# Retention with a decay split per key and per query, one root for three norms, and the fourth retrieval in one piece

## The chip, the cores and the metric

The kernel runs on one core of a Trainium2 chip. The metric is the device time of one execution in microseconds (us). TensorE (PE) does matmuls, VectorE (DVE) and ScalarE (ACT) elementwise work and reductions, GpSimd (POOL) issues the indirect DMAs that gather expert rows, and SyncE (SP) issues the plain ones. The engines run side by side and wait for each other through semaphores.

## What is computed

A decoder layer over 512 tokens of width 1024: a mixer of four retention heads and four differential attention heads, a layer norm, then PEER, a retrieval of 128 of 16384 experts per token (8 heads, 16 each), and a second layer norm. Cut to what matters:

```python
# retention, per head, chunks of 128 tokens, g the head's decay
s = (q_i k_j^T) * decay_in          # g^(i-j), 0 for i < j
out = s v_j + (q_i state) * decay_q # state: all earlier chunks, decayed
r = silu(gate) * GroupNorm(out)     # eps 1e-5, over the 128 values of a head
# attention
a = softmax(q1 k1^T) - lam * softmax(q2 k2^T)
d = 0.8 * RMSNorm(a v)
x = LayerNorm(alpha * x + concat(r, d) @ W_out)
# PEER, per token
top = top16 of the sums of two top16 lists of 128 key scores
h = gelu(x . U[expert]);  y = sum(softmax(score) * h * V[expert])
x = LayerNorm(alpha * x + y)
```

## The kernel before

The 512 tokens are four blocks of 128, one token per partition. Block 0 goes ahead alone: projections, retention, attention, layer norm and its retrieval. From then on GpSimd gathers the experts of block 0, while TensorE does projections, retention and attention of blocks 1 to 3. At last come the queries and retrieval of these blocks, and the gather of their 384 experts per partition.

**The gather of block 0.** An expert's row is 4 KB of U and 4 KB of V; one indirect DMA brings one row for each of the 128 tokens (512 KB). `U k` is a group of four such transfers, rows 4k to 4k+3 (here "rows"), and `V j` likewise. They land in a ring of 16 slots, four quads A to D, and a slot is filled anew only when its row has been used (`slot_used`). GpSimd issues in the fixed order of `ROWS`: U0 to U19 in quads A and B by turns; then, once the last retention product is done (`ret_mixed` 4, since quads C and D lie in buffers of the retention), V0 U20 V1 U21 V2 U22 V3 U23 V4 U24 U25 V5 U26 U27 V6 U28 U29 U30 V7 U31 V8 V12 V9 V13 and so on. From there V0 to V11 use C and A by turns, even U use D, odd U use B, V12 uses D, V13 B. VectorE takes each U row with a dot product with x (`dot`, L1120, 128x1024), in order, wherever its program says `rows(n)`. V0 to V11 are summed by TensorE (`add_rows`, L529) with a diagonal matrix of weights that ScalarE makes (L964); V12 and later by VectorE (`weighed_sum`, L1134).

**Projections of blocks 1 to 3.** The order is rotated queries and keys (RQ, RK), RV, the gate RG, then DQ, DKK, DV for attention, the last three as 4 + 4 + 3 fills. A fill waits until its bank, used three fills before, has been read: the second and third DQ fill wait for VectorE's gate (`swish_gate`, L1264) of blocks 2 and 3. Beside the rotations and gates VectorE takes rows and the retrievals 2 and 3 of block 0: the loop counter `i` runs over nine fills, retrieval 2 stands at i = 5, and `best_keys(0, 3)` alone at i = 6, behind the first gate. Between the DQ, DKK and DV fills TensorE does retention: scores of query block b against key block jb into ACC (L710), and the product with v into W[:, 3] (L720), in the steps of the list `RETENTION`.

**Retention on VectorE.** `decay_scores` scales each tile of scores with a table that holds the whole decay g^(i-j); tiles two or three blocks off the diagonal take four instructions, one for each head. `retention_norm` of a block has statistics, a root by three Newton steps, the norm of four heads out of PSUM, gain, bias and the gate. It stands behind each block's product, and the product of the next block waits for it (`ret_normed`), since all use one bank. Then `weights(0)` makes the first V weights from the gelu that ScalarE has computed ahead of its last projection copy.

**Attention.** For each block b and head h VectorE masks the scores and takes their maximum (`softmax_max`), takes `BESIDE_HEAD[b]` rows, and joins the two softmaxes (`softmax_join`). In block 1, heads 1 and 2 have one row each, beside `best_pairs` and `best_experts` of the fourth retrieval. For blocks 2 and 3, head 2 has two rows and the layer norm `ln1` of the block before. After the heads come four rows, `diff_norm(b)` and `AFTER_NORM[b]` rows. TensorE has for each head the scores of the next head, one V group (block 1: V0 to V3, and V4 behind the heads), the transposes of this head's probabilities, and the product; the last row of the V group stands between transposes and product. A block ends with the turning of the normed mix (L783) and the scores of the next block.

## Time and profile before

| | us |
|---|---|
| median of 3 runs | 1594.28 (1594.04 to 1595.39) |
| profiled execution | 1593.78 |
| its span | 1592.0 |
| busy PE / DVE / ACT / POOL | 1288.4 / 1123.6 / 271.6 / 737.2 |
| DMA | 603.45 MB, mean 379 GB/s |

The profiled execution is 0.5 us under the median, and 1.8 us of it lie outside the span from the first to the last instruction. Busy shares are means over the whole span. An engine that is idle for half of it can still be the one that all wait for in a stage, so the table is read together with windows of time and the idle time in front of an instruction.

### The profile page before, as it was taken

The numbers are of one execution on the slowest core, as the hardware profiler recorded it, in microseconds if no ns is written. First come the engines' busy times: TensorE is split into PE (matmuls) and PEld (weight loads), VectorE is DVE, ScalarE is ACT, GpSimd is POOL, SyncE is SP. The second block draws the span as 40 slices with busy tenths as digits, with TensorE's granted clock in tenths as the row PEclk, the third lists the DMA queues.
The fourth block names the chain that finished last, engine by engine and source line by source line (L and its number), as shares of the span: only waits on it lengthen the run. The fifth ranks groups of instructions, "written<-read, shape, count | busy, mean of one in ns | idle before, by whom it ended". The sixth has DMA issues, their size and how long they took to land.

```text
span 1592.0 us, 11574 instructions
## 1 busy us (share of the span) xinstructions
PE 1288.4 (81%) x3512; PEld 619.0 (39%) x3512; DVE 1123.6 (71%) x2626; ACT 271.6 (17%) x771; POOL 737.2 (46%) x645
## 2 busy tenths in 40 slices
PE   8999989977678995788787777778787868778787
PEld 5466446433334563333233333333333323333232
DVE  1459999777787967987676768676767686755555
ACT  0200100212122110121212121212121212121111
POOL 0006475767656456454444443535353444344430
PEclk9999989998889998899989898979998899899988
DMA  9859898989889989999999999999999999999994
GB/s 349 352 216 390 296 364 298 412 289 341 286 295 348 351 329 416 381 421 422 421 422 422 421 421 421 422 422 421 421 422 421 421 422 421 422 421 422 421 422 177
DMA packets 100254, 603.45 MB, mean 379 GB/s; under 512 B 11616, under 2 KB 11872, under 8 KB 47584
## 3 DMA queue, kind: packets, MB, share of 16 engines
q0 software_dynamic: 92160, 536.91, 83.7%
q1 hardware_dynamic: 8032, 65.80, 10.3%
q8 instruction: 28, 0.46, 0.1%
q14 instruction: 34, 0.28, 0.0%
HBM read 600.57 MB, written 2.10 MB: 379 GB/s over the span
## 4 chain that ended last, share of the span: by engine, by line
DMA 43%; PE 22%; DVE 21%; POOL 7%; issue 4%; ACT 1%; SPq 1%; DVEq 0%; POOLq 0%
DMA arena<-uv,idx 41%; PE W L542 7%; POOL arena L505 5%; DVE arena L1142 4%; PE ACC L542 4%; PE W L580 3%; PE W L586 3%; PE W L828 2%; DVE arena L1120 2%; DVE xs L1134 2%; DMA arena<-w_in 1%; PE ACC L529 1%; PE X L664 1%; PE X L795 1%; DVE cand L1405 1%
## 5 line engine op out<-in xcount | busy, mean ns | idle before, releaser
L1142 DVE SCALAR_TENSOR_TENSOR arena<-arena,xs 128x1024 f32<-128x1024 f32 x384 | 466.9, 1226 | 293.2 <-DMA arena<-uv,idx 291.4
L489 POOL DMA_INDIRECT arena<-uv,idx x384 | 426.8, 1112 | 530.2 <-PE W L542 310.8
L542 PE MATMUL W<-arena,fdiag 128*128 128x512 f32 x1024 | 494.2, 642 | 144.0 <-ACT fdiag L1072 143.9
L505 POOL DMA_INDIRECT arena<-uv,idx x232 | 282.0, 1216 | 265.3 <-DVE idx L1412 116.9
L542 PEld LDWEIGHTS W<-arena,fdiag 128*128 128x128 f32 x1024 | 206.9, 206 | 430.7 <-issue 249.7
L542 PE MATMUL ACC<-arena,fdiag 128*128 128x512 f32 x512 | 252.8, 655 | 70.4 <-ACT fdiag L1072 70.3
L542 PEld LDWEIGHTS ACC<-arena,fdiag 128*128 128x128 f32 x512 | 105.6, 210 | 217.5 <-issue 131.5
L1072 ACT ACTIVATE fdiag<-ident,gate 128x128 f32<-128x128 f32 x384 | 123.6, 390 | 340.1 <-DVE gate L1150 329.8
L1120 DVE SCALAR_TENSOR_TENSOR arena<-arena,xs 128x1024 f32<-128x1024 f32 x128 | 150.4, 1223 | 22.2 <-DMA arena<-uv,idx 20.8
L580 PE MATMUL W<-arena 128*128 128x512 f32 x272 | 122.7, 605 | 8.7 <-DMA arena<-w_in 8.1
L1134 DVE SCALAR_TENSOR_TENSOR xs<-arena,gate,xs 128x1024 f32<-128x1024 f32 x80 | 102.7, 1284 | 33.4 <-DMA arena<-uv,idx 26.5
L828 PE MATMUL W<-arena 128*128 128x128 f32 (+1 forms) x512 | 112.7, 381 | 1.5 <-ACT arena L1014 1.5
L1064 ACT ACTIVATE hid<-hid 128x4 f32<-128x4 f32 (+2 forms) x101 | 20.7, 205 | 427.5 <-DVE arena L1142 427.5
L828 PEld LDWEIGHTS W<-arena 128*128 128x128 f32 x512 | 77.4, 191 | 35.8 <-ACT arena L1014 2.0
L580 PEld LDWEIGHTS W<-arena 128*128 128x128 f32 x272 | 51.5, 194 | 69.1 <-issue 65.6
L586 PE MATMUL W<-arena 128*128 128x128 f32 (+1 forms) x256 | 61.5, 399 | 7.8 <-issue 4.3
L529 PE MATMUL ACC<-arena,fdiag 128*128 128x512 f32 x96 | 47.5, 645 | 9.1 <-DMA arena<-uv,idx 6.3
L586 PEld LDWEIGHTS W<-arena 128*128 128x128 f32 x256 | 40.3, 199 | 26.5 <-issue 13.3
L795 PE MATMUL X<-arena 128*128 128x512 f32 x96 | 47.1, 641 | 1.6 <-issue 1.6
L1142 DVE DVE_READ_ACCUMULATOR arena<-arena,xs 128x1 f32 x384 | 31.6, 82 | 0.0
L529 PEld LDWEIGHTS ACC<-arena,fdiag 128*128 128x128 f32 x96 | 18.9, 206 | 31.3 <-issue 24.1
L1031 ACT ACTIVATE arena<-W 128x384 f32<-128x384 f32 (+1 forms) x20 | 10.2, 512 | 116.1 <-PE W L828 109.6
(198 smaller groups left out, 896.6 us busy)
## 6 DMA issues: line engine op xcount, KB each, us to landing
arena<-w_in SPq DMA_DIRECT2D x13, 2048.0 KB, 18.6
arena<-peer_w_query SPq DMA_DIRECT2D x8, 2048.0 KB, 19.8
arena<-uv,idx POOLq DMA_INDIRECT x616, 29.1
arena<-w_out SPq DMA_DIRECT2D x4, 2048.0 KB
arena<-w_in SPq DMA_DIRECT2D x4, 512.0 KB, 6.7
arena<-xT SPq DMA_DIRECT2D x1, 1536.0 KB, 11.8
xs<-x SPq DMA_DIRECT2D x1, 1536.0 KB, 14.6
out<-xs SPq DMA_DIRECT2D x3, 512.0 KB
```

The costliest lines, as they stand in the source:

```text
L489: pool.indirect_dma_start(out=fused[slot], out_offset=None, in_=uv, in_offset=bass.IndirectOffsetOnAxis(ap=idx[:, E + n:E + n + 1], axis=0 ...
L505: pool.indirect_dma_start(out=ring[r], out_offset=None, in_=rows, in_offset=bass.IndirectOffsetOnAxis(ap=idx[:, e:e + 1], axis=0), element ...
L529: last = nc.tensor.matmul(ACC[:, half * HW:(half + 1) * HW], fdiag[:, i % ND, :], ring[r][:, half * HW:(half + 1) * HW], start=i == 0, sto ...
L542: last = nc.tensor.matmul(sum_of(b)[:, half * HW:(half + 1) * HW], fdiag[:, n % ND, :], fused[n % NS][:, D + half * HW:D + (half + 1) * HW ...
L580: last = nc.tensor.matmul(bank, act_T(k, part * P, (part + 1) * P), wts[slot][:, k, :], start=(k == 0), stop=(k == KD - 1))
L586: last = nc.tensor.matmul(bank[:, at:at + n_tok], wts[slot][:, k, h * P:(h + 1) * P], act_T(k, toks.start, toks.stop), start=(k == 0), sto ...
L795: last = nc.tensor.matmul(X_BANKS[half], mixT[:, k, :], wts[slot_of_out(half)][:, k, :], start=(k == 0), stop=(k == KD - 1))
L828: last = nc.tensor.matmul(dst, wts[slot][:, k, i * P:(i + 1) * P], act_T(k, toks.start, toks.stop), start=(k == 0), stop=(k == KD - 1))
L1072: nc.scalar.activation(fdiag[:, n % ND, :], ident[:], ACT.Copy, scale=gate[:, E + n:E + n + 1]).then_inc(pair_diag_ready, 1)
L1120: STT(out=ring[r], in0=ring[r], scalar=1.0, in1=xs[:, 0, :], op0=ALU.mult, op1=ALU.mult, accum_out=hid[:, e:e + 1]).then_inc(slot_used[r], 1)
L1134: STT(out=xs[:, 0, :], in0=ring[r], scalar=gate[:, e:e + 1], in1=xs[:, 0, :], op0=ALU.mult, op1=ALU.add).then_inc(slot_used[r], 1)
L1142: STT(out=fused[slot][:, 0:D], in0=fused[slot][:, 0:D], scalar=1.0, in1=xs[:, b, :], op0=ALU.mult, op1=ALU.mult, accum_out=hid[:, E + n:E ...
```

## The change

Four things are changed.

- The decay g^(i-j) is split. The factor of the query is left out, since a norm follows that divides each row by its own size, and the norm's epsilon is multiplied by the square of what was left out (`row_eps`). What remains depends on the key alone: on the diagonal a table with the mask (`near`, still VectorE's), off it one number per key and head (`across`), which ScalarE applies as the scale of a copy (`scale_scores`, 24 pieces of 128x128 behind copies of projections).
- The products of blocks 1, 2 and 3 go to three banks (`RET_BANKS`), so none waits for a norm. VectorE takes only statistics for each, then one root for all three. ScalarE applies scale and bias in 12 pieces of 128x128, behind its last projection copy, and VectorE multiplies by gain, adds the bias and gates in three instructions over 1536 elements (`retention_gate`). The first maximum of attention stands behind these.
- The fourth retrieval of block 0 stands whole at i = 6, between the first two gates.
- The rows are dealt out anew: 28 in place of 24 beside retention, 5 beside each head of blocks 1 and 2 (2 at head 2 of block 2), none after the norm of block 1.

```diff
-BESIDE_HEAD = {1: 5, 2: 6, 3: 4}
-AFTER_NORM = {1: 8, 2: 3, 3: 11}
+BESIDE_HEAD = {1: 5, 2: 5, 3: 4}
+AFTER_NORM = {1: 0, 2: 3, 3: 11}
...
+        near = part(5 * K, HW)
+        across = part(5 * K + HW, 3 * H, "p (o h) -> p o h", o=3)
+        eps_in = part(5 * K + HW + 3 * H, H)
...
+        row_eps = sb("row_eps", [P, H])
+        ret_mv = work[:, 0:6 * H].rearrange("p (q h c) -> p q h c", q=3, h=H)
+        ret_scale = work[:, 6 * H:9 * H]
+        ret_bias = work[:, 9 * H:12 * H]
+        ret_root = work[:, 12 * H:18 * H].rearrange("p (i n) -> p i n", i=2)
+        ret_out = attn[:, :].rearrange("p (q n) -> p q n", q=3)
...
+        RET_BANKS = [W[:, 3, :], X_BANKS[0], X_BANKS[1], W[:, 3, :]]
...
-                        pe.wait_ge(ret_decayed, tiles_before(NB))
+                        pe.wait_ge(ret_decayed, NB)
+                        pe.wait_ge(ret_scaled, tiles_before(NB - 1))
                     pe.wait_ge(row_landed[r], landed(p))
...
             def retention_mix(b):
-                pe.wait_ge(ret_decayed, tiles_before(b + 1))
-                if b > 1:
-                    pe.wait_ge(ret_normed, b)
+                pe.wait_ge(ret_decayed, b + 1)
+                if b:
+                    pe.wait_ge(ret_scaled, tiles_before(b))
                 for h in range(H):
                     for jb in range(b + 1):
-                        last = nc.tensor.matmul(W[:, 3, h * P:(h + 1) * P], sT[:, jb, h * P:(h + 1) * P],
+                        last = nc.tensor.matmul(RET_BANKS[b][:, h * P:(h + 1) * P], sT[:, jb, h * P:(h + 1) * P],
                                                 rv[:, jb, h * P:(h + 1) * P], start=(jb == 0), stop=(jb == b))
                 last.then_inc(ret_mixed, 1)
...
                     pe.wait_ge(a_ready, n + 1)
                     if b == 1 and h == 0:
-                        pe.wait_ge(ret_normed, NB)
+                        pe.wait_ge(ret_applied, 1)
                     else:
...
+                    for b, jb in OFF_TILES.get(fill[0] - 1 - fill_of(1, RG) - 1, ()):
+                        scale_scores(b, jb)
+                act.wait_ge(ret_scales_ready, 1)
+                for q in range(3):
+                    for h in range(H):
+                        n = q * H + h
+                        last = nc.scalar.activation(ret_out[:, q, h * P:(h + 1) * P], RET_BANKS[q + 1][:, h * P:(h + 1) * P],
+                                                    ACT.Identity, bias=ret_bias[:, n:n + 1], scale=ret_scale[:, n:n + 1])
+                last.then_inc(ret_applied, 1)
+            OFF_TILES = {1: [(1, 0)], 3: [(2, 0), (2, 1)], 6: [(3, 0), (3, 1)], 7: [(3, 2)]}
+            def scale_scores(b, jb):
+                act.wait_ge(ret_scored, tiles_before(b) + jb + 1)
+                act.wait_ge(ret_mixed, b)
+                if b == 1:
+                    act.wait_ge(proj_taken_dve, takes(len(FILLS), "dve"))
+                src = ACC[:, jb % 2 * HW:(jb % 2 + 1) * HW]
+                for h in range(H):
+                    last = nc.scalar.activation(sT[:, jb, h * P:(h + 1) * P], src[:, h * P:(h + 1) * P], ACT.Copy,
+                                                scale=across[:, b - jb - 1, h:h + 1])
+                last.then_inc(ret_scaled, 1)
...
-            def decay_scores(b, jb):
-                off = b - jb
-                dve.wait_ge(ret_scored, tiles_before(b) + jb + 1)
-                src = ACC[:, jb % 2 * HW:(jb % 2 + 1) * HW]
-                if off < 2:
-                    TT(out=sT[:, jb, :], in0=src, in1=dec[:, off, :], op=ALU.mult).then_inc(ret_decayed, 1)
-                else:
-                    for h in range(H):
-                        ins = STT(out=sT[:, jb, h * P:(h + 1) * P], in0=src[:, h * P:(h + 1) * P],
-                                  scalar=decay_far[h] ** (off - 1), in1=dec[:, 1, h * P:(h + 1) * P],
-                                  op0=ALU.mult, op1=ALU.mult)
-                    ins.then_inc(ret_decayed, 1)
...
-            def retention_norm(b):
-                R = W[:, 3, :]
-                q = b - (b > 0)
-                dve.wait_ge(ret_mixed, b + 1)
+            def decay_scores(b):
+                dve.wait_ge(ret_scored, tiles_before(b) + b + 1)
+                src = ACC[:, b % 2 * HW:(b % 2 + 1) * HW]
+                TT(out=sT[:, b, :], in0=src, in1=near, op=ALU.mult).then_inc(ret_decayed, 1)
+            def retention_norm_0():
+                R = RET_BANKS[0]
+                dve.wait_ge(ret_mixed, 1)
                 links([nc.vector.bn_stats(st[:, h, :], R[:, h * P:(h + 1) * P]) for h in range(H)])
                 links([nc.vector.bn_aggr(mv[:, h, :], st[:, h, :]) for h in range(H)])
-                link(TS(rstd[:], mv[:, :, 1], EPS, None, ALU.add))
-                inverse_root(rstd[:], H)
+                link(TT(out=rstd[:], in0=mv[:, :, 1], in1=row_eps[:], op=ALU.add))
+                inverse_root(rstd[:], H, root)
                 for h in range(H):
                     ins = TS(work[:, h * P:(h + 1) * P], R[:, h * P:(h + 1) * P], mv[:, h, 0:1], rstd[:, h:h + 1],
                              ALU.subtract, ALU.mult)
-                    if h == H - 1:
-                        ins.then_inc(ret_normed, 1)
-                dve.wait_ge(ret_normed, b + 1)
+                ins.then_inc(ret_normed, 1)
+                dve.wait_ge(ret_normed, 1)
                 link(TT(out=work[:, 0:HW], in0=work[:, 0:HW], in1=gn[:, 0, :], op=ALU.mult))
                 link(TT(out=work[:, 0:HW], in0=work[:, 0:HW], in1=gn[:, 1, :], op=ALU.add))
-                if b:
-                    link(TT(out=swish[:, q, :], in0=work[:, 0:HW], in1=swish[:, q, :], op=ALU.mult))
+            def retention_statistics(b):
+                R = RET_BANKS[b]
+                dve.wait_ge(ret_mixed, b + 1)
+                links([nc.vector.bn_stats(st[:, h, :], R[:, h * P:(h + 1) * P]) for h in range(H)])
+                links([nc.vector.bn_aggr(ret_mv[:, b - 1, h, :], st[:, h, :]) for h in range(H)])
+            def retention_scales():
+                by_block = ret_scale.rearrange("p (q h) -> p q h", q=3)
+                link(TT(out=by_block, in0=ret_mv[:, :, :, 1], in1=row_eps[:].unsqueeze(1).to_broadcast([P, 3, H]), op=ALU.add))
+                inverse_root(ret_scale, 3 * H, ret_root)
+                STT(out=ret_bias.rearrange("p (q h) -> p q h", q=3), in0=ret_mv[:, :, :, 0], scalar=-1.0, in1=by_block,
+                    op0=ALU.mult, op1=ALU.mult).then_inc(ret_scales_ready, 1)
+            def retention_gate():
+                dve.wait_ge(ret_applied, 1)
+                for i, op in ((0, ALU.mult), (1, ALU.add)):
+                    link(TT(out=ret_out, in0=ret_out, in1=gn[:, i, :].unsqueeze(1).to_broadcast([P, 3, HW]), op=op))
+                link(TT(out=swish[:], in0=ret_out, in1=swish[:], op=ALU.mult))
...
-                if i == 5:
-                    retrieve(0, 2)
-                elif i == 6:
-                    best_keys(0, 3)
+                if i in (5, 6):
+                    retrieve(0, i - 3)
             dve.wait_ge(rot_turned, rots(len(FILLS)))
             rows(HALF)
-            for b in range(1, NB):
-                for jb in range(b + 1):
-                    decay_scores(b, jb)
-                    if jb % 2:
-                        rows(HALF)
-                if b > 1:
-                    rows(HALF)
-                retention_norm(b)
+            decay_scores(1)
+            rows(HALF)
+            retention_statistics(1)
+            rows(HALF)
+            decay_scores(2)
+            rows(HALF)
+            retention_statistics(2)
+            rows(HALF)
+            decay_scores(3)
+            rows(2 * HALF)
+            retention_statistics(3)
+            retention_scales()
             weights(0)
+            rows(HALF)
+            retention_gate()
             for b in range(1, NB):
                 for h in range(H):
                     softmax_max(b, h)
                     if b > 1 and h == 2:
                         rows(2)
                         ln1(b - 1)
-                    elif (b, h) == (1, 1):
-                        best_pairs()
-                        rows(1)
-                    elif (b, h) == (1, 2):
-                        best_experts(0, 3)
-                        rows(1)
                     else:
...
-    decay = (np.stack([near, far], axis=1) * P ** -0.5).reshape(P, 2, HW)
+    left = np.exp((P - 1 - i)[:, None] * log_g[None, :]) * P ** -0.5
+    near = (i[None, None, :] >= i[:, None, None]) * left[:, :, None]
+    across = left[:, None, :] * np.exp(P * np.arange(1, NB)[None, :, None] * log_g[None, None, :])
+    row_eps = EPS * np.exp(2.0 * (P - 1 - i)[:, None] * log_g[None, :])
+    decay = np.concatenate([near.reshape(P, -1), across.reshape(P, -1), row_eps], axis=1)
     ang = np.arange(S)[:, None] * (10000.0 ** (-np.arange(64) / 64.0))[None, :]
     rope = np.stack([np.cos(ang), np.sin(ang)]).reshape(2, NB, P, 64).transpose(2, 0, 1, 3).reshape(P, -1)
```

On VectorE between the gates of blocks 1 and 2, before (L1264 is the gate, L1375 to L1379 `best_keys`, L1120 the dots):

```order
L1264 SCALAR_TENSOR_TENSOR arena<-arena,W 128x512
L1375 MAX best_v<-arena 128x8 x4
L1376 MATCH_REPLACE cand<-best_v,arena 128x128 x4
L1377 MAX_INDEX best_i<-best_v,arena 128x8 x4
L1378 MAX best_v<-cand 128x8 x4
L1379 MAX_INDEX best_i<-best_v,cand 128x8 x4
L1120 SCALAR_TENSOR_TENSOR arena,hid<-arena,xs 128x1024 x8
```

And the same place after the change, from the last step of `best_keys` to the second gate (L1433 to L1442 `best_pairs`, L1449 to L1461 `best_experts`):

```order
L1428 MAX_INDEX best_i<-best_v,cand 128x8 x4
L1433 TENSOR_TENSOR cand<-best_v 128x512
L1438 MAX top_v<-cand 128x8 x2
...
L1452 TENSOR_TENSOR cand<-pos_u,iota_f 128x1024
L1454 TENSOR_TENSOR cand<-cand,best_i 128x1024
L1455 TENSOR_REDUCE sel<-cand 128x64
...
L1461 SCALAR_TENSOR_TENSOR idx<-sel 128x32
L1160 SCALAR_TENSOR_TENSOR arena,hid<-arena,xs 128x1024 x8
L1304 SCALAR_TENSOR_TENSOR arena<-arena,W 128x512
```

The eight dots and the second and third gate now stand behind thirteen more kinds of instruction.

On VectorE at the end of retention, before (L1296 to L1304 end the norm of block 3, L1168 to L1172 are `weights(0)`, L1310 begins attention):

```order
L1296 TENSOR_SCALAR arena<-W,mv,rstd 128x128 x4
L1301 TENSOR_TENSOR arena<-arena 128x512
L1302 TENSOR_TENSOR arena<-arena 128x512
L1304 TENSOR_TENSOR arena<-arena 128x512
L1168 TENSOR_REDUCE gsum<-gate 128x4
L1169 RECIPROCAL gsum<-gsum 128x4
L1170 TENSOR_TENSOR gate<-gate,gsum 128x64
L1172 TENSOR_TENSOR gate<-gate,hid 128x64
L1310 TENSOR_TENSOR W<-W,mask 128x2x128
```

And after the change (L1345 makes the biases of the norms, L1352 and L1353 are `retention_gate`):

```order
L1345 SCALAR_TENSOR_TENSOR arena<-arena 128x12
L1208 TENSOR_REDUCE gsum<-gate 128x4
L1209 RECIPROCAL gsum<-gsum 128x4
L1210 TENSOR_TENSOR gate<-gate,gsum 128x64
L1212 TENSOR_TENSOR gate<-gate,hid 128x64
L1160 SCALAR_TENSOR_TENSOR arena,hid<-arena,xs 128x1024 x4
L1352 TENSOR_TENSOR arena<-arena 128x1536 x2
L1353 TENSOR_TENSOR arena<-arena 128x1536
L1359 TENSOR_TENSOR W<-W,mask 128x2x128
```

Four dots and the gate of all three blocks now stand between the weights and the first maximum.

On ScalarE after the change, at the end of the projections (L931 a projection copy, L1088 and L1091 the exponential and gelu for `weights(0)`, L977 the norm's pieces, L1014 the first exponentials of attention):

```order
L931 ACTIVATE arena<-W 128x512 x2
L1088 ACTIVATE gate<-gate 128x64
L1091 ACT_TABLE_LOAD
L1091 ACTIVATE hid<-hid 128x64
L931 ACTIVATE arena<-W 128x512
L977 ACTIVATE arena<-X,arena 128x128 x8
L977 ACTIVATE arena<-W,arena 128x128 x4
L1014 ACT_TABLE_LOAD
L1014 ACTIVATE arena,zsum<-W,nmax 128x256 x2
```

The twelve pieces are new. They stand behind the copy of the last projection and ahead of the table load of attention.

## Rows read from the trace of the kernel before

**Rows 1.** The page: chain of waits that ended last, by engine.

```profile
DMA 43%; PE 22%; DVE 21%; POOL 7%; issue 4%; ACT 1%; SPq 1%; DVEq 0%; POOLq 0%
```

**Rows 2.** Windows: stretch, length; PE, PEld, DVE, ACT, POOL busy; clock, DMA share, GB/s.

```profile
229.00:297.70 68.70, 68.57 (x272) 42.81 (x272) 59.51 (x159) 5.82 (x11) 45.76 (x37) 0.96 0.90 340
...
300.60:361.60 61.00, 46.08 (x128) 21.51 (x128) 49.90 (x118) 13.41 (x50) 39.73 (x34) 0.91 0.87 326
361.60:432.90 71.30, 50.24 (x136) 24.08 (x136) 54.57 (x119) 15.51 (x46) 51.62 (x43) 0.86 0.86 310
...
570.00:1580.00 1010.00, 794.46 (x1726) 343.43 (x1725) 684.63 (x1593) 183.26 (x535) 445.99 (x403) 0.90 1.00 414
```

**Rows 3.** Timeline of TensorE: start, length, line, operation, idle before and releaser.

```profile
215.95 7.09 PE L586 MATMUL W<-arena 128*128 128x384 f32 x16 [3.45 <-DVE arena L1264]
...
229.13 7.89 PE L586 MATMUL W<-arena 128*128 128x384 f32 x16 [4.31 <-issue]
...
302.32 5.40 PE L529 MATMUL ACC<-kT,fdiag 128*128 128x512 f32 x8
...
309.49 1.88 PE L529 MATMUL ACC<-rv,fdiag 128*128 128x512 f32 x4
...
355.55 1.04 PE L783 MATMUL W<-ident,arena 128*128 128x128 f32 x8
```

**Rows 4.** Timeline of VectorE: the fourth retrieval and what follows its parts.

```profile
308.72 0.75 DVE L1384 TENSOR_TENSOR cand<-best_v 128x512 f32<-128x512 f32 x1
...
313.84 1.22 DVE L1120 SCALAR_TENSOR_TENSOR arena<-arena,xs 128x1024 f32<-128x1024 f32 x1
...
317.49 0.26 DVE L1400 TENSOR_SCALAR pos_u<-top_p 128x32 uint32<-128x32 uint32 x2
317.79 1.23 DVE L1403 TENSOR_TENSOR cand<-pos_u,iota_f 128x1024 f32<-128x1024 uint32 x1
...
322.11 1.22 DVE L1120 SCALAR_TENSOR_TENSOR arena<-arena,xs 128x1024 f32<-128x1024 f32 x1
```

**Rows 5.** Timeline of VectorE: a norm of retention, then tiles of the next block.

```profile
239.27 0.89 DVE L1291 BATCH_NORM_STATS2 st<-W 128x6 f32<-128x128 f32 x4
...
240.60 0.17 DVE L1293 TENSOR_SCALAR rstd<-mv 128x4 f32<-128x4 f32 x1
...
243.00 1.37 DVE L1296 TENSOR_SCALAR arena<-W,mv,rstd 128x128 f32<-128x128 f32 x4
...
246.58 0.88 DVE L1281 SCALAR_TENSOR_TENSOR arena<-ACC,arena 128x128 f32<-128x128 f32 x4
247.38 0.68 DVE L1277 TENSOR_TENSOR arena<-ACC,arena 128x512 f32<-128x512 f32 x1
```

**Rows 6.** Timeline of ScalarE: four diagonals of V0.

```profile
301.53 1.27 ACT L964 ACTIVATE fdiag<-ident,gate 128x128 f32<-128x128 f32 x4
```

**Rows 7.** Timeline of GpSimd: transfers, with idle time before and releaser.

```profile
284.87 0.98 POOL L505 DMA_INDIRECT kT<-uv,idx  x1 [0.30 <-issue]
...
323.61 0.93 POOL L505 DMA_INDIRECT arena<-uv,idx  x1 [7.33 <-DVE arena L1120]
327.25 1.68 POOL L505 DMA_INDIRECT arena<-uv,idx  x1 [2.71 <-DVE arena L1120]
...
385.07 0.94 POOL L505 DMA_INDIRECT arena<-uv,idx  x1 [0.30 <-issue]
...
405.43 1.68 POOL L505 DMA_INDIRECT arena<-uv,idx  x1 [7.17 <-DVE arena L1120]
...
561.53 1.73 POOL L489 DMA_INDIRECT arena<-uv,idx  x1 [16.01 <-DVE idx L1412]
```

**Rows 8.** Timeline of VectorE: three waits in attention.

```profile
346.40 0.17 DVE L1347 TENSOR_SCALAR rstd<-ssq 128x4 f32<-128x4 f32 x1 [9.02 <-ACT arena L998]
...
390.65 1.22 DVE L1120 SCALAR_TENSOR_TENSOR arena<-arena,xs 128x1024 f32<-128x1024 f32 x1 [1.66 <-DMA arena<-uv,idx]
...
445.77 4.06 DVE L1134 SCALAR_TENSOR_TENSOR xs<-arena,gate,xs 128x1024 f32<-128x1024 f32 x3 [4.34 <-DMA arena<-uv,idx]
```

35 lines of the change are left out of this document (19 added, 16 removed).

## The prediction

> **What bounds the kernel now.** I read four views. The chain of waits says where time can be given back: transfers of expert rows hold 43% of it, TensorE 22%, VectorE 21% [rows 1]. The table of windows then gives the stages. From 570 us on the DMA engines are full to the end (share 1.00 over 1010 us, 414 GB/s [rows 2]), and the bytes are fixed. So the end moves with one instant: the issue of the first row of block 1, at 561.53 us, for which GpSimd had waited 16.01 us [rows 7]. What the change can do is move that instant. It is reached through attention of blocks 1, 2 and 3, then layer norm and queries, a chain that the change doesn't touch behind 433 us.
>
> Ahead of it the timelines of each engine matter, because no engine is full everywhere. From 229 to 297.7 TensorE has 68.57 us of work in 68.70 us [rows 2], and its start there, at 229.13 us, follows an idle 4.31 us for which the row names no engine; the fill reuses the bank of the last gate, as the one at 215.95 us, behind 3.45 us of waiting for VectorE, reuses that of the gate before [rows 3]. In attention of block 1, GpSimd stops for 7.33 and 2.71 us at 323.61 and 327.25 us, since VectorE does retrieval instead of using rows; TensorE then lacks V rows and VectorE waits 9.02 us at 346.40 us [rows 7, 8]. There is another stop of 7.17 us at 405.43 us [rows 7].
>
> **The change on VectorE.** Removed: three norms of 7.3 us (239.27 to 246.58 [rows 5]), 21.9 us; the scaling of the six off-diagonal tiles, three in four instructions (0.88 us in all) and three in one (0.68 us [rows 5]), less overlap about 4.2 us. Added: three times statistics (239.27 to 240.60, 1.3 us), 3.9 us; one root over 12 columns, as long as the one over 4, with bias, 2.6 us (240.6 to 243.0 plus one step [rows 5]); three operations over 1536 elements. The trace has 1.23 us for 1024 elements [rows 4], so about 1.8 us each, 5.4 us. The saving is 26.1 - 11.9 = 14.2 us. Row dots are only moved: both kernels have done 128 of them by the norm of block 2.
>
> **The fourth retrieval.** Its pairs (308.72 to 313.84, 5.1 us) and experts (317.49 to 322.11, 4.6 us) [rows 4] leave attention of block 1, and stand between the first and second gates of block 1 to 3. That is 9.7 us ahead of the last gate, on which TensorE waits. Ends: +9.7 us if the loop "row used, next transfer issued, landed" moves as a whole; +6.3 us if all landings are then hidden, because eight dots of 1.15 us are 9.2 us, where the stretch from gate to gate took 13.2 us (215.95 to 229.13 [rows 3]), 0.7 us of it a gate. A transfer needs 5.6 us from issue to landing (385.07 to 390.65 [rows 7, 8]), and since the first of the eight is issued only when the first of the eight before it is used, the 3.4 us of landing waits mostly stay; I take +9.0 us. TensorE has no gap behind it to absorb this. It ends the projections at 297.7 + 9.0 = 306.7 us, and the last retention product, which frees the buffers of the V rows, moves from 284.87 [rows 7] to 293.9 us. VectorE's 14.2 us are not lost to work but to waiting: its diagonal tiles of blocks 2 and 3 must wait for TensorE's scores, which now come 9 us later, while VectorE comes earlier. ScalarE's six scaled tiles are 24 pieces, 7.6 us by [rows 6], where it has 5.82 us of work in 68.7 us [rows 2]; each is behind the copy of a projection and done within 2.6 us, while TensorE is in the next projection of over 5 us. I cost them at nothing; without that cover it would be up to 2.6 us for each of three blocks.
>
> **The new wait.** ScalarE applies the three norms behind its last projection copy, so not before TensorE's 306.7 us, although the scales are ready at about 297 us (third product 293 us, statistics 1.3, root 2.6). Copy 0.6 us, then 12 pieces. Nearest row: four scaled copies of the same size in 1.27 us [rows 6], so 3.8 us; bounds 2.4 us (0.2 each, under the rate of that row) and 6 us (0.5 each). ScalarE is done at 311.1 us. VectorE is held at retention_gate, has 5.4 us there, and behind it is queued the first maximum of attention, for which TensorE, ScalarE and the V rows wait. It ends at 316.5 + 1.4 = 318 us against 300.6 us: 17.4 us late.
>
> A rule of the Trainium skill bears on this price: "ScalarE: Activation LUTs", section "What ACT_TABLE_LOAD costs", has 186 ns and 0.833 ns per column for an activation, 93 ns more for each per-partition operand, and an overlap of 93 ns. For one such operand that makes 1.27 us for four, as the row; the new pieces have two, a scale and a bias, and would need 4.7 us, which would put all that follows 0.9 us later.
>
> **Attention of block 1.** GpSimd's order of transfers is unchanged: V0 U20 V1 U21 V2 U22 V3 U23 V4 U24 U25. V0 starts at 293.9, U21 is out at about 315 us. V2 takes the slots of V0, and TensorE takes V0 only behind the first maximum: 1.7 us behind it, 5.40 us for two rows and 1.88 us for each further one [rows 3]. So V2 goes out from 324 to 330 us: a stop of some 8 us, in the place of the 7.33 and 2.71 us that go. From then on the heads run in lockstep with the stream. Each head now wants five new U rows, up to a group that is issued behind V(h+2), whose last slot is freed behind the join of head h: 2.3 us (transposes and one V row of 1.88 us), one issue and one to three more of 1.25 us, landing 5.6 us, a dot and a join of 2.4 us: 12.9, 14.2 and 15.4 us, against the 8.8 us of a head before (308.72 and 317.49, behind the second and third maximum [rows 4]). Joins end at 325, 338, 352 and 367 us. U25, four rows on, lands by 373 us; norm 3.6 us. V4 on TensorE (four rows, 7.2 us) ends at 382.5 us, and from the turning at 355.55 us [rows 3] to the maximum at 361.6 us it was 6.0 us: block 2 starts at 388.5 us, 26.9 us late, with four dots more behind it.
>
> **Attention of block 2.** Before: 71.3 us, of which VectorE was busy 54.57 us [rows 2]. Four dots fewer are 50.0 us, and rows now lie ready because the stream has gone on: 388.5 + 50.0 = 438.5 us, 5.6 us late where it was 26.9. The stop of 7.17 us at the layer norm gets shorter too, since all of U28 is used ahead of it (BESIDE_HEAD 5 and four rows in hand).
>
> **Attention of block 3.** Before, VectorE waits there 4.34 us for V rows at 445.77 us [rows 8]. The stream at that place (V8, V9, V12, V13) is late by 0 to 2 us only, so the wait takes up 4.3 of the 5.6 us; TensorE, late by some us more, gives back a part. I take +2 us, which goes through 561.53 us to the end. The profiled execution took 1593.78 us; with +2 us it is 1595.8. The median of the runs shown, 1594.28, is 0.5 us above it: 1596.3 us.
>
> Bounds of this case: with +6.3 us in place of +9.0 the delay at 433 us is 2.9 us and is wholly taken up, about -0.5 us in all. If TensorE is still at the V row before when a head's join comes, its last one is freed 1.9 us later [rows 3], and the three heads cost 5 us more: +6 us. So 1593.8 to 1600.5 us.
>
> **Rivals.**
> Stream first, faster. If GpSimd doesn't stop for V2 and the heads don't hold it, the stream starts 9 us late (V0), but drops the stops of 7.33, 2.71 and most of 7.17 us: 9 - 17 = -8 us, 1586 us. For it: the DMA share in 300.6 to 432.9 us is only 0.87 and 0.86 [rows 2], so up to 18 us are there to be had, and the freed VectorE time is 14.2 us. Against it: V2 can't be issued until V0 is used, and that is behind the wait for ScalarE.
>
> Start of attention not given back, slower. The wait of 4.34 us in block 3 takes up the delay only if V12 and V13 aren't late. They reuse slots of the last U rows, dotted in block 2. If the lockstep lasts into block 2 (V5 and V6 wait for heads of it, and V7 is summed ahead of the turning), these slots are freed 6 to 8 us late, and nothing is taken up: 1601.5 us. It decides once block 2 ends over 6 us late.
>
> The saving counts in full: VectorE's 14.2 us go straight into the chain, 1580 us. Only 21% of the chain is VectorE's, and TensorE's full stretch speaks against it.
>
> **How the numbers follow.** Forecast 0.50 (of it 0.39 same, 0.09 slower, 0.02 faster); stream first 0.24; not given back 0.23; in full 0.03. What this measurement can tell from no change is 0.2%, 3.2 us. Of each of the first two rivals 0.03 is same. Faster: 0.21 + 0.03 + 0.02 = 0.26. Same: 0.39 + 0.06 = 0.45. Slower: 0.20 + 0.09 = 0.29. The range goes from 1586.5 to 1602 us.
>
> **What would show it.** TensorE's last projection at 304 to 307 us instead of 297.7; ScalarE's 12 pieces behind it, 3 to 5 us; VectorE idle at retention_gate for some 4 us and the first maximum at 315 to 318 us; GpSimd stopped for TensorE near 320 us and not for VectorE; heads of 12 to 15 us; block 2 from 380 or later; a shorter wait than 4.34 us in block 3; the first row of block 1 at 562 to 566 us. It is wrong if block 2 starts before 372 us, if the last gate is late by less than 5 us, or if the time from 570 us on changes.

## The result, and the profile after

The changed kernel takes 1610.27 us (median of 4 runs, 1607.85 to 1610.74) against 1594.49 us of the kernel before beside it: ratio 1.0099, 95% interval 1.0087 to 1.0112. It is 15.8 us slower where I had forecast +2, and lies above my range. The profiled execution took 1607.85 us, its span is 1605.9, so the traces have 13.9 us of the loss. All ratios of this document leave out one execution of 1620.94 us, of the kernel before with the retrieval moved, which was in a slower state of the chip; the median of 1600.18 us given for that kernel counts it (1599.63 without).

The windows of the changed kernel, cut at the last projection, the gate, the first maximum of block 2, the norm of block 2 and the first row of block 1 (columns as in [rows 2]):

```profile
229.00:303.70 74.70, 71.72 (x296) 45.32 (x294) 52.64 (x118) 12.93 (x36) 48.63 (x44) 0.98 0.96 353
303.70:314.00 10.30, 0.70 (x4) 0.30 (x4) 5.93 (x6) 6.06 (x14) 7.66 (x6) 0.68 1.01 418
314.00:391.00 77.00, 51.67 (x128) 23.86 (x128) 41.40 (x93) 13.53 (x50) 42.55 (x42) 0.80 0.81 292
391.00:444.00 53.00, 45.44 (x136) 21.86 (x136) 50.41 (x113) 15.40 (x46) 35.85 (x29) 0.94 0.84 292
444.00:575.00 131.00, 113.09 (x356) 58.87 (x355) 109.06 (x185) 25.93 (x65) 74.31 (x66) 0.95 0.86 321
575.00:1605.00 1030.00, 806.03 (x1759) 350.23 (x1757) 699.52 (x1619) 184.24 (x537) 456.39 (x408) 0.90 0.99 409
```

Attention of block 1 lasts 77 us where it had 61 [rows 2], and VectorE works 41.40 us of it instead of 49.90. The retrieval's 9.7 us have left this stage, so VectorE has less to do here and is idle for 35.6 us where it was for 11.1. From 575 us on the DMA engines are full, as in [rows 2].

GpSimd in the changed kernel, start, length and idle before each transfer (the stops, the rows issued behind them, and the first row of block 1):

```profile
290.21 0.94 POOL L517 DMA_INDIRECT kT<-uv,idx  x1 [2.15 <-PE W L737]
...
321.53 0.97 POOL L517 DMA_INDIRECT kT<-uv,idx  x1 [8.64 <-PE ACC L542]
...
342.27 0.93 POOL L517 DMA_INDIRECT arena<-uv,idx  x1 [4.77 <-PE ACC L542]
343.51 0.94 POOL L517 DMA_INDIRECT arena<-uv,idx  x1 [0.30 <-issue]
...
345.99 0.94 POOL L517 DMA_INDIRECT arena<-uv,idx  x1 [0.30 <-issue]
...
359.24 0.94 POOL L517 DMA_INDIRECT rv<-uv,idx  x1 [6.99 <-PE ACC L542]
...
425.37 0.94 POOL L517 DMA_INDIRECT arena<-uv,idx  x1 [2.71 <-PE ACC L542]
...
452.18 0.94 POOL L517 DMA_INDIRECT arena<-uv,idx  x1 [0.30 <-issue]
...
575.52 1.74 POOL L501 DMA_INDIRECT arena<-uv,idx  x1 [15.66 <-DVE idx L1461]
```

The two stops for VectorE in block 1 (7.33 and 2.71 us in [rows 7]) are gone, and the one of 7.17 us in block 2 has shrunk to 0.89 and 1.97 us (402.57 and 412.21). In their place GpSimd waits for TensorE: for the first slot of V2 (321.53), then for the last slot of V3, of V4 and of V5 (2.48 us at 377.48), and in block 2 for the last slot of V7 (425.37), behind which it issues without a stop up to the first row of V13 (452.18). The first row of block 1 comes at 575.52 us, 13.99 late: the instant that the prediction had named carries the loss.

VectorE in the changed kernel, the gate and the waits:

```profile
308.52 3.55 DVE L1352 TENSOR_TENSOR arena<-arena 128x1536 f32<-128x1536 f32 x2 [4.26 <-ACT arena L977]
312.11 1.76 DVE L1353 TENSOR_TENSOR arena<-arena 128x1536 f32<-128x1536 f32 x1
313.90 0.43 DVE L1359 TENSOR_TENSOR W<-W,mask 128x256 f32<-128x256 f32 x1
...
333.77 1.22 DVE L1160 SCALAR_TENSOR_TENSOR arena<-arena,xs 128x1024 f32<-128x1024 f32 x1 [6.86 <-DMA arena<-uv,idx]
...
348.82 1.23 DVE L1160 SCALAR_TENSOR_TENSOR arena<-arena,xs 128x1024 f32<-128x1024 f32 x1 [7.13 <-DMA arena<-uv,idx]
...
352.53 1.22 DVE L1160 SCALAR_TENSOR_TENSOR arena<-arena,xs 128x1024 f32<-128x1024 f32 x1 [1.09 <-DMA arena<-uv,idx]
353.69 0.16 DVE L1368 RECIPROCAL rz<-zsum 128x2 f32<-128x2 f32 x1
...
365.70 1.23 DVE L1160 SCALAR_TENSOR_TENSOR arena<-arena,xs 128x1024 f32<-128x1024 f32 x1 [8.29 <-DMA arena<-uv,idx]
...
390.77 0.43 DVE L1359 TENSOR_TENSOR W<-W,mask 128x256 f32<-128x256 f32 x1 [7.75 <-PE W L753]
...
442.86 1.13 DVE L1399 SCALAR_TENSOR_TENSOR arena<-W,rstd,arena 128x128 f32<-128x128 f32 x4
446.87 2.67 DVE L1174 SCALAR_TENSOR_TENSOR xs<-arena,gate,xs 128x1024 f32<-128x1024 f32 x2 [2.88 <-DMA arena<-uv,idx]
...
458.12 1.29 DVE L1174 SCALAR_TENSOR_TENSOR xs<-arena,gate,xs 128x1024 f32<-128x1024 f32 x1 [4.06 <-DMA arena<-uv,idx]
```

The wait for ScalarE (4.26 us) and the gate stand ahead of the first maximum. Then each of three heads has one long wait for a U row. Block 3's wait for V rows, 4.34 us in [rows 8], is still 4.06 us although VectorE comes 12 us later.

### The profile page after: what moved, and what is told of

The parts are those of the page before. It is cut to its first block, busy times and chain, and to the rows that moved or that the text cites. A ratio compares the mean times of both kernels' runs of the same rounds, so it can differ in the third digit from the quotient of the medians.

```text
span 1605.9 us, 11561 instructions
## 1 busy us (share of the span) xinstructions
PE 1291.9 (80%) x3512; PEld 620.7 (39%) x3512; DVE 1110.9 (69%) x2571; ACT 282.2 (18%) x807; POOL 732.0 (46%) x645
## 3 DMA queue, kind: packets, MB, share of 16 engines
q1 hardware_dynamic: 8032, 65.55, 10.2%
## 4 chain that ended last, share of the span: by engine, by line
DMA 43%; PE 26%; DVE 20%; POOL 4%; issue 3%; ACT 2%; SPq 1%; DVEq 0%; POOLq 0%
DMA arena<-uv,idx 42%; PE W L555 8%; DVE arena L1182 4%; POOL arena L517 3%; PE ACC L555 3%; PE ACC L542 3%; PE W L593 3%; PE W L845 2%; PE W L599 2%; PE X L812 2%; DVE arena L1160 2%; DVE xs L1174 2%; DMA arena<-w_in 1%; PE X L677 1%; DVE top_p L1439 1%
## 5 line engine op out<-in xcount | busy, mean ns | idle before, releaser
L555 PEld LDWEIGHTS ACC<-arena,fdiag 128*128 128x128 f32 x512 | 106.8, 213 | 217.4 <-issue 133.3
L599 PE MATMUL W<-arena 128*128 128x128 f32 (+1 forms) x256 | 62.0, 401 | 15.4 <-DVE arena L1304 15.4
L753 PE MATMUL W<-dkT,arena 64*128 64x256 f32 (+2 forms) x48 | 13.2, 632 | 25.4 <-ACT arena L1014 23.2
L1071 ACT ACTIVATE arena<-W 128x384 f32<-128x384 f32 (+1 forms) x20 | 10.2, 512 | 116.1 <-PE W L845 116.1
## 6 DMA issues: line engine op xcount, KB each, us to landing
xs<-x SPq DMA_DIRECT2D x1, 1536.0 KB, 14.2
```

Source lines behind the costliest of these rows:

```text
L555: last = nc.tensor.matmul(sum_of(b)[:, half * HW:(half + 1) * HW], fdiag[:, n % ND, :], fused[n % NS][:, D + half * HW:D + (half + 1) * HW ...
L599: last = nc.tensor.matmul(bank[:, at:at + n_tok], wts[slot][:, k, h * P:(h + 1) * P], act_T(k, toks.start, toks.stop), start=(k == 0), sto ...
```

## The experiments

Theory GROUP, formed from these rows: U groups of four rows are issued in the order U20 V1 U21 V2 U22 V3 U23 V4 U24. A head's dots need the rows up to some group. With 80 rows used ahead of attention and 5 beside each head, head h (0 to 3) reads into U(21+h). For heads 1 to 3 that group is issued behind V(h+1), which takes the slots of V(h-1), and the last of these is freed behind the join of head h-1. So each head waits until the join before it has passed through TensorE, GpSimd and a landing. (The expectations count from the head whose join frees the slot, and so say V(h+2).) With 76 rows ahead a head reads into U(20+h), one group less. The rivals: START (the late first maximum passes whole to the end), ROWS or HEADS (five rows beside a head are too many anyway), DECAY (the decays and norms on ScalarE cost it).

Each ratio below is to the kernel before, run on the same chip. The chips differ between groups of experiments, and a ratio can be 0.1% off the quotient of the two medians (1606.88 by 1596.76 gives 1.0063 where the ratio is 1.0049), so differences of that size are not read. "Moved retrieval" means pairs and experts of the fourth quarter.

**Undoing one part, or doing it alone.** First, retrieval and rows of block 1 as before:

```diff
-                if i in (5, 6): retrieve(0, i - 3)
+                if i == 5: retrieve(0, 2)
+                elif i == 6: best_keys(0, 3)
+                    elif (b, h) == (1, 1): best_pairs(); rows(1)
+                    elif (b, h) == (1, 2): best_experts(0, 3); rows(1)
-AFTER_NORM = {1: 0, 2: 3, 3: 11}
+AFTER_NORM = {1: 8, 2: 3, 3: 11}
```

> The changed kernel (median 1610.27) with its fourth retrieval put back where it was: best keys between the first two gates, pairs and experts beside the second and third head of block 1; the rows beside those heads and behind the norm go back with it (5, 1, 1, 5, 8), everything else of the change stays. Theory START (the late start of attention, 14.7 us at the first maximum, goes through whole; about 6 of it come from the retrieval ahead of the last gate and 8.7 from the norms that wait for ScalarE): last projection at 297, first maximum at 307 to 309, and a time of 1602 to 1604. Theory HEADS (the five rows beside each head of block 1 wait for transfers; the start matters little): heads as before, 1593 to 1597. Theory DECAY (the scaled tiles and norms on ScalarE cost the time): no gain, 1608 or more.

Measured: 1592.92 us, ratio 0.9976 (0.9952 to 1.0000), against 1.0099. START can't be the whole: its first maximum comes 7.3 us late (306.51 against 299.22), and its time is no longer than that of the kernel before. (The profiled execution, 1596.71 us, is a long one of this kernel: its block 3 begins at 435.40 us, 2.95 early, and its first row comes at 564.55, 3.0 late; the last section has 2.6 us of what lies between.) DECAY fell: the new decays and norms are in it.

The other way round, the kernel before with the retrieval moved and the rows of block 1 dealt 5 and 0:

> The kernel before (median 1594.5) with only the fourth retrieval moved in one piece between the first two gates, and rows dealt as in the changed kernel in block 1 (5 beside each head, none behind the norm). Decays and norms are the old ones. START: the last projection ends 6 to 9 us late, so does the first maximum, and that goes through: 1600 to 1604. HEADS: lockstep heads on top of it, the whole loss of the change is here: 1607 to 1611. DECAY: 1593 to 1597.

Measured: 1600.18 us, ratio 1.0031 (0.9998 to 1.0065). That is at the low edge of START, since the kernel before had 1596.76 on this chip. But this move costs only some 5 us here by the ratio (3.4 by the medians, and the interval reaches 1), and undoing it in the changed kernel gained over 15. The effects don't add; something in the changed kernel makes it dear. The difference is that the changed kernel has used 80 rows ahead of attention, and this one 76. Adding them ahead, and taking them from block 2 as the change does:

```diff
             weights(0)
+            rows(HALF)
             for b in range(1, NB):
-BESIDE_HEAD = {1: 5, 2: 6, 3: 4}
+BESIDE_HEAD = {1: 5, 2: 5, 3: 4}
```

> The kernel before with the fourth retrieval in one piece and all of the changed kernel's dealing of rows (80 rows ahead of attention, 5 beside each head of blocks 1 and 2, none behind the norm of block 1); decays and norms are the old ones. It differs from the one-piece kernel measured at 1600.2 against 1596.8 by those four rows. GROUP: heads of block 1 go from 11 us to 14 to 17 and the time to 1606 to 1610 by the scale on which the kernel before has 1596.8. START: the first maximum moves by at most 2 us, so does the time: 1600 to 1603. A time like the changed kernel's (over 1609) would mean that the new decays and norms cost nothing and bring nothing.

Measured: 1606.84 us against 1593.61, ratio 1.0085 (1.0056 to 1.0113). Its first maximum (309.72) is only 2.7 us later than with 76 rows (307.06), its last join of block 1 begins 29 us later (374.88 against 345.94). With old decays and norms this is nearly all of the loss.

**The same four rows in the changed kernel.**

```diff
             weights(0)
-            rows(HALF)
             retention_gate()
-AFTER_NORM = {1: 0, 2: 3, 3: 11}
+AFTER_NORM = {1: 4, 2: 3, 3: 11}
```

> The changed kernel with four row dots taken from ahead of attention (behind the statistics of block 3) and put behind the norm of block 1: 76 rows are used before the first maximum, as in the kernel before, instead of 80. Retrieval, decays and norms stay as changed. Theory GROUP (80 rows ahead plus five beside each head make every head of block 1 need a group of U rows whose transfers are issued behind V(h+2), a V row whose slot comes free behind the join of the head itself; with 76 each head needs one group less): waits for DMA in the heads fall from about 7 to 2 to 4.5 us, the heads from 15 to 18 us to 11 to 12, the maximum of block 2 from 390.8 to 375 to 381, time 6 to 11 below the changed kernel, 1600 to 1605 by the clock of its first measurement (kernel before 1594.5). Theory START (only the late first maximum counts): time within 2 us of the changed kernel. Theory ROWS (five rows beside each head are too many, wherever one starts): heads stay at 15 us or more, within 2 us too.

Measured: 1601.55 us, ratio 1.0050 (1.0030 to 1.0070). Four dots, moved and not saved, give back a third to a half of the loss (0.0025 of the 0.0075 that the changed kernel has in its second measurement below, 0.0049 of the 0.0099 in its first). VectorE's waits in the heads of this kernel:

```profile
340.01 1.23 DVE L1160 SCALAR_TENSOR_TENSOR arena<-arena,xs 128x1024 f32<-128x1024 f32 x1 [3.40 <-DMA arena<-uv,idx]
350.70 1.23 DVE L1160 SCALAR_TENSOR_TENSOR arena<-arena,xs 128x1024 f32<-128x1024 f32 x1 [3.04 <-DMA arena<-uv,idx]
361.81 1.23 DVE L1160 SCALAR_TENSOR_TENSOR arena<-arena,xs 128x1024 f32<-128x1024 f32 x1 [4.45 <-DMA arena<-uv,idx]
```

They were 6.86, 7.13 and 8.29 us; the first maximum of block 2 comes at 375.69 us instead of 390.77. GROUP holds. ROWS, by which the five beside a head stay too many, falls.

GROUP says more: with 80 rows ahead and 4 beside each head the last groups read are the same as with 76 and 5. With the changed kernel again beside it:

> The changed kernel with 4 rows beside each head of block 1 in place of 5 and the 4 rows so taken behind its norm; the 80 rows ahead of attention stay. Theory GROUP: what counts is the last group of U rows that a head reads (head h then reads U(20+h), as with 76 rows ahead and 5 beside each, where the ratio was 1.005; the changed kernel's heads read U(21+h)): waits for DMA of 2 to 5 us in a head instead of 7, block 2's first maximum at 373 to 380, ratio 1.003 to 1.006. Rival AHEAD (80 rows used before attention drain the ring, and the rows beside a head don't matter): ratio 1.008 or more. Rival ROWS (only the number beside a head matters): 1.000 to 1.003, below the kernel with four rows later.

> The changed kernel itself again, on the chip of the three kernels that run beside it, so that they can be compared with it directly. A ratio to the kernel before of 1.009 to 1.011, as at first (1.0099).

Measured: 1595.42 us, ratio 1.0017 (1.0003 to 1.0032), and the changed kernel 1605.95 us, 1.0075 (1.0051 to 1.0098), below the 1.009 to 1.011 that I expected of it. AHEAD fell clearly, and the first maximum of block 2 (374.64 us) is where GROUP put it. The ratio is below what I expected of GROUP and within that of ROWS (1.000 to 1.003), so one row less beside a head is worth some more than its group. How much can't be said: the interval meets that of the kernel with four rows later, at 1.0030.

**Place of the retrieval, and of the norms.** Pairs and experts can stand where VectorE waits for TensorE in any case:

```diff
             rows(HALF)
+            best_pairs()
             decay_scores(2)
 ...
             rows(HALF)
+            best_experts(0, 3)
             decay_scores(3)
```

> The changed kernel with pairs and experts of the fourth retrieval taken from between the gates and put into two stretches in which VectorE waits for TensorE's retention scores (4.66 us at 257.80 and 7.88 us at 279.54); best keys stay ahead of the last gate, rows as in the changed kernel. START: last gate 7 us earlier, last projection at 297, first maximum at 307 to 309, time 1602 to 1604, as with the old place of the retrieval. HEADS: five rows beside each head stay, so the heads stay in lockstep with the transfers and little is gained: 1607 to 1610. The two kernels with the retrieval out of the gates differ under HEADS by 10 us and under START by less than 2.

Measured: 1601.43 us, ratio 1.0020 (1.0001 to 1.0040). Nearer to START than to HEADS, and by the ratio below both, though the heads stayed in lockstep: waits of 7.58, 7.05 and 8.39 us, block 2 at 387.15 us. So the retrieval ahead of the gate costs some us of its own: by the traces 4.8 at the first row (570.76 against 575.52), by the ratios more (0.0055 to 0.0079). What is left, 0.0044 against the old retrieval (0.9976), is the dealing of block 1 together with the place of pairs and experts; no run here parts the two.

ScalarE's twelve pieces ahead of its last projection copy:

```diff
                     if fill[0] == len(FILLS) - 1:
                         gelu_0(0)
+                        apply_norms()
                     take_fill(1, WAVES[1])
```

> The changed kernel with ScalarE's twelve norm pieces issued ahead of its last projection copy instead of behind it, so that they lie beside TensorE's last projection. START: pieces at about 299 to 304, three operations of VectorE behind them, first maximum at 309 to 310.5 instead of 313.9, time 3.5 to 4.5 lower, 1606 to 1607. HEADS: the heads wait for transfers all the same, under 1.5 us gained, 1609 or more. DECAY: like START, since the wait is ScalarE's.

Measured: 1606.88 us, ratio 1.0049 (1.0018 to 1.0079). From the last projection's end to the first maximum it was 10.2 us (303.67 to 313.90); here it is 5.8 (307.72 to 313.52), the 4.4 us foreseen. Against the changed kernel's two measurements, 1.0075 and 1.0099, the gain is 0.0026 and 0.0050, where START had 0.0022 to 0.0028. The interval overlaps that of the first of these and not that of the second, so the size stays open. In the profiled execution TensorE was 4 us later to begin with, and the first row comes 1.7 us earlier (573.81 against 575.52). The same edit where the heads are free:

> The changed kernel with the retrieval and the rows of block 1 put back as before, and ScalarE's twelve norm pieces ahead of its last projection copy. The first maximum comes 4.4 us earlier than without the latter (306.5), at 302. GROUP: no lockstep in these heads, so VectorE sets them and the 4.4 us count at least in part: 2 to 4.5 us below the kernel with only the old retrieval, which is 6 to 8 us below the kernel before (ratio 0.995 to 0.996). START: 4.4 us in full. The rival DECAY, by which the new norms bring nothing, has it within 2 us of the kernel before.

Measured: 1585.36 us, ratio 0.9949 (0.9934 to 0.9963): 4.3 us (0.0027) below the same without the edit, as expected, though the two intervals still meet, and clearly faster than the kernel before.

**Together.** The retrieval in the waits, the norms earlier, the four rows behind the norm:

> Three edits of the changed kernel at once: pairs and experts of the fourth retrieval in VectorE's waits of the retention stage, the norm pieces ahead of ScalarE's last copy, and the four row dots behind the norm of block 1. First maximum at 302. GROUP: heads of about 10 to 11 us, block 2 from 352 to 358, 5 to 9 us below the kernel before (ratio 0.9945 to 0.997). ROWS: five rows beside each head hold the heads at 15 us or more: at or above the kernel before. START: 1594 to 1597 by the scale on which the kernel before has 1594.5.

Measured: 1586.49 us, ratio 0.9952 (0.9936 to 0.9967). Then with fewer rows beside each head (`BESIDE_HEAD` 4 and 3 for block 1, `AFTER_NORM` 8 and 12):

> The kernel with the retrieval in the waits, the norms earlier and 76 rows ahead (ratio 0.9952), with 4 rows beside each head of block 1 and 8 behind its norm in place of 5 and 4. Head h then reads U(19+h). GROUP: the waits of 4.17, 2.52 and 3.71 us in its heads shrink to under 2 us each, but the rows come behind the norm instead, where TensorE's V4 lies beside them: 0 to 4 us lower, ratio 0.993 to 0.9955. Rival TAIL (what the heads gain is lost at the V rows that block 3 needs): same within 1 us.

> The same with 3 rows beside each head and 12 behind the norm. GROUP: no wait for DMA in the heads, which last as long as their V rows on TensorE, 8.3 us; behind the norm VectorE has 12 dots, 14 us, beside TensorE's V4 and block 2's first scores, and is now the later: block 2's first maximum at 352 to 358; ratio 0.991 to 0.996, no clear difference from 4 and 8.

Measured: with 4 rows 1581.20 us, ratio 0.9924 (0.9901 to 0.9947); with 3 rows 1584.88 us, 0.9947 (0.9931 to 0.9963). The version with 4 is 12.2 us faster than the kernel before and the lowest of the three; its interval meets those of the other two, so the order among them isn't settled. VectorE's waits of over 0.5 us for U rows in it, from the first maximum of block 1 to the end of block 2:

```profile
336.53 1.23 DVE L1164 SCALAR_TENSOR_TENSOR arena<-arena,xs 128x1024 f32<-128x1024 f32 x1 [4.10 <-DMA arena<-uv,idx]
339.85 1.22 DVE L1164 SCALAR_TENSOR_TENSOR arena<-arena,xs 128x1024 f32<-128x1024 f32 x1 [0.67 <-DMA arena<-uv,idx]
347.75 1.22 DVE L1164 SCALAR_TENSOR_TENSOR arena<-arena,xs 128x1024 f32<-128x1024 f32 x1 [1.95 <-DMA arena<-uv,idx]
364.87 1.22 DVE L1164 SCALAR_TENSOR_TENSOR arena<-arena,xs 128x1024 f32<-128x1024 f32 x1 [4.40 <-DMA arena<-uv,idx]
381.35 1.23 DVE L1164 SCALAR_TENSOR_TENSOR arena<-arena,xs 128x1024 f32<-128x1024 f32 x1 [3.52 <-DMA arena<-uv,idx]
```

All come behind the last join of block 1, whose joins begin 7.4 to 8.4 us apart (307.99 to 331.07). With 3 rows the heads have no wait for a transfer either, and block 2 starts at 360.15 us instead of 358.84, later than the 358 that I gave as a bound; which of its waits sets that I did not settle.

**Does block 3's wait take up a delay?** Eight operations without effect (128x512, `max(x, x)`) were put into the kernel before on VectorE, ahead of the first maximum of block 3, or of block 2; and seven of 1024 elements ahead of the very first:

```diff
             for b in range(1, NB):
+                for _ in range(8 if b == 3 else 0):
+                    link(STT(out=work[:, 0:512], in0=work[:, 0:512], scalar=1.0, in1=work[:, 0:512], op0=ALU.mult, op1=ALU.max))
```

> The kernel before with eight operations of no effect on VectorE (128x512, 5.3 us in all by the 1.23 us of one over 1024 elements), put behind the norm of block 2 and its three V rows, ahead of the first maximum of block 3. All dots of block 2 are done in time. Theory SLOTS (the wait at 445.77 us takes up a delay as long as the rows it waits for were issued in time): nearly all taken up, ratio 1.000 to 1.001. Rival NEVER (the wait moves along with VectorE in any case, since the V rows of block 3 wait for VectorE or TensorE again): the 5.3 us go through, ratio 1.003 to 1.0035.

> The kernel before with the same eight operations ahead of the first maximum of block 2, so that all dots of block 2 and the slots that they free come 5.3 us late, less the wait for TensorE or DMA that stands at that place anyway. SLOTS: the V rows of block 3 are issued late by as much, nothing is taken up in block 3; what reaches the end is what block 2's own waits (6.08, 1.66 and 0.61 us for DMA) leave: ratio 1.001 to 1.0033, and above that of the delay put behind block 2 by at least 0.001. NEVER: no difference between the two beyond 0.0005.

> The kernel before with seven operations of no effect over 1024 elements on VectorE (8.6 us) ahead of the first maximum of attention, less the 4.5 us for which it waits there for TensorE: the first maximum at about 303.5 to 304 instead of 299.2. Retrieval and rows stay where they were. GROUP: no head needs a group behind V(h+2), so the delay is partly taken up in the waits of 9.02 and 6.08 us: ratio 1.000 to 1.002. Rival START (goes through whole): 1.0027 or more.

Measured: 1597.12, 1601.60 and 1600.15 us against 1596.37; ratios 1.0004 (0.9986 to 1.0022), 1.0018 (0.9993 to 1.0043), 1.0010 (0.9985 to 1.0034). The medians stand as SLOTS has them, but the intervals don't separate anything. The traces do. In that of the late start the first maximum comes 4.5 us late (303.73), block 3 begins 4.1 us late (442.47) and the first row of block 1 3.6 us (565.08): a plain late start passes for the most part, against what I expected of GROUP. VectorE with the delay behind block 2's dots:

```profile
439.21 5.77 DVE L1485 SCALAR_TENSOR_TENSOR arena<-arena 128x512 f32<-128x512 f32 x8
445.01 0.43 DVE L1310 TENSOR_TENSOR W<-W,mask 128x256 f32<-128x256 f32 x1
...
446.83 5.46 DVE L1134 SCALAR_TENSOR_TENSOR xs<-arena,gate,xs 128x1024 f32<-128x1024 f32 x4
452.21 0.16 DVE L1319 RECIPROCAL rz<-zsum 128x2 f32<-128x2 f32 x1
```

and with it ahead of them:

```profile
440.45 0.42 DVE L1310 TENSOR_TENSOR W<-W,mask 128x256 f32<-128x256 f32 x1
...
447.57 2.69 DVE L1134 SCALAR_TENSOR_TENSOR xs<-arena,gate,xs 128x1024 f32<-128x1024 f32 x2 [4.04 <-DMA arena<-uv,idx]
...
451.80 0.16 DVE L1319 RECIPROCAL rz<-zsum 128x2 f32<-128x2 f32 x1
```

In the first the wait is gone: the four V rows run without a break. The join begins 2.46 us late (452.21 against 449.75), of which 0.86 were there ahead of the eight operations (439.21 against 438.35), so 1.6 of their 5.77 us pass. In the second, block 2 itself has taken up most, but the 2.1 us that come out of it meet a wait of 4.04 us, nearly whole, and the join is 2.05 us late. So the wait takes up what comes behind block 2's dots, and nothing of what comes ahead of them.

GpSimd's rows say why, and not quite as SLOTS has it. The first row of V13, for which VectorE waits, isn't held by its own slot: in the kernel before U31's first dot frees that slot at about 424 us, and the row is issued at 439.55. It is held by the order of issue. The last stop ahead of it is the one of 7.17 us at 405.43, which ends with a dot of the fourth head of block 2; from there on GpSimd issues row after row. With the delay behind the dots this stop ends at 406.61 us and V13 is issued at 440.40, while VectorE comes 5.77 us later. With the delay ahead of them the stop ends at 407.21 and V13 is issued at 441.64, 2.09 us late, as late as the join.

Behind that join the second trace loses 6 us more, up to a first row at 569.77 us (8.24 late); 2.6 of them are in the last section, and where the others arise is open. So its time of 1602.12 us is no measure of the delay.

## Why the prediction was wrong

The instants of VectorE's first masked maximum in each block, and of the first row of block 1, in us:

| kernel | block 1 | block 2 | block 3 | first row | ratio |
|---|---|---|---|---|---|
| before | 299.22 | 360.06 | 438.35 | 561.53 | 1 |
| changed | 313.90 | 390.77 | 450.98 | 575.52 | 1.0099 |
| before, retrieval moved | 307.06 | 372.34 | 444.51 | 567.35 | 1.0031 |
| the same, 80 rows ahead | 309.72 | 391.81 | 451.82 | 574.83 | 1.0085 |
| changed, four rows later | 316.24 | 375.69 | 444.64 | 568.77 | 1.0050 |
| fastest | 302.14 | 358.84 | 427.43 | 550.13 | 0.9924 |

- The last projection 9 us late: right. The first profile of the changed kernel has 303.67 us, +6.0, since its front part ran 2.7 us ahead (first gate 197.42 against 200.14); seven profiles with the retrieval ahead of the gate have 303.67 to 309.28, mean 306.8 (predicted 306.7), and those without it 296.3 to 299.1. From the first gate to the end of the last projection it was 106.25 us instead of 97.57, 8.7 more.
- The new wait: right in mechanism and size. Twelve pieces took 4.29 us (304.20 to 308.49), between my 3.8 and the 4.7 of the Trainium skill's rule for two pointer operands ("ScalarE: Activation LUTs", section "What ACT_TABLE_LOAD costs"), which is 0.4 us high here. The gate took 5.3 us (predicted 5.4), VectorE's wait 4.26, and the first maximum came 14.7 us late where I had 17.4, the 2.7 being the front part again.
- Lockstep heads: right in mechanism, too small in size. From join to join it was 15.7, 17.1 and 18.1 us (320.90, 336.62, 353.69, 371.74) instead of 12.9, 14.2, 15.4. Between the second and third join, V3's last slot was freed 4.2 us behind the join (about 338.05 to 342.27) where I had 2.3, and U23's third row needed 6.5 us from issue to landing (345.99 to 352.53), where I had 5.6. Of the first, 1.4 us are the clock, shown below.
- Block 2 in 50.0 us: nearly right, 51.7 (from the end of its first maximum at 392.3 us to 444.0). But it began 3.8 us later than predicted, so it ended 11.1 us late and not 5.6.
- **The step that failed: "the wait of 4.34 us in block 3 takes up 4.3 of the 5.6 us", since "the stream at that place (V8, V9, V12, V13) is late by 0 to 2 us only".** The stream was late by all of it: V8 by 10.6 us (432.70 against 422.10), V13 by 12.6 (452.18 against 439.55), and the wait was still 4.06 us. The table shows it again: 6.2 us late at block 3 are 5.8 at the first row, 6.3 are 7.2. What held the stream was TensorE. V7 reuses the slots of V5, and V5 is summed beside the third head of block 2, so V7's last row could go only at 425.37, 0.3 us behind the last row of V5, and all behind it in the order of issue moved along:

```profile
416.04 5.42 PE L542 MATMUL ACC<-arena,fdiag 128*128 128x512 f32 x12
...
423.21 1.88 PE L542 MATMUL ACC<-arena,fdiag 128*128 128x512 f32 x4
```

In the kernel before, V5 had been summed by 406.85 us and V7's last row went at 414.83 without a wait. What I had as a rival, "start of attention not given back", is what happened, and its condition (block 2 more than 6 us late) was met. But its reason was only half right. It had V7 behind TensorE, and then V12 and V13 held by the slots of the last U rows. Those slots were free: U31's first dot began at 434.94 us and ended 16 us before V13's first row was issued.
- In numbers: the prediction had +5.6 us at the end of block 2 and +2 at the first row of block 1. The trace has 11.1 and 13.99. So 5.5 of the 12 us by which I missed are the size of the lockstep (3.8) and of block 2 (1.7); of the other 6.5, 3.6 are the step above, which I had as taken up, and 2.9 were added between 444 us and 575.52: 1.4 of them by a longer wait for the late stream (2.88 us at 446.87, where the kernel before has 1.50), the rest I can't assign. The rival's price, 7.2 us in all, was too low because block 2 alone already ended 11.1 us late. The rival "stream first" failed at its condition: GpSimd did stop for V2, for 8.64 us.
- I had also taken the row dots as "only moved". That they were moved across a boundary between groups is what made the heads wait: 0.0054 of the time in the kernel before (1.0031 to 1.0085), 0.0025 to 0.0049 in the changed one. VectorE's saving could be had. With retrieval and rows of block 1 as before, the kernel with the new decays and norms was 3.8 us below the kernel before (an interval that reaches 1), and with the norms earlier 8.3 us, clear of noise.

## What to carry over

Where two streams of transfers share one queue, count for each consumer the last group that it reads, and follow that group's place in the issue order back to the slot that frees it: four rows more or fewer ahead of the loop can cost as much as all the arithmetic saved is worth (here some 8 us). A wait for a transfer takes up a delay only if the queue has passed its last stop ahead of that transfer before the delayed work; if the delayed work, or what follows it on another engine, ends that stop, the wait moves along. The stop can be many transfers ahead (here V7's, 17 ahead of V13's first), while the slot of the transfer itself has long been free. Put work that was cut out of one stage where an engine waits anyway (here the 4.66 and 7.88 us of the retention stage), not ahead of something for which the engine without a gap waits. Here that gave back 4.8 us at the first row.
